# Differential attention: the low halves of eight weight chunks made by GpSimd in a stream of its own instead of by VectorE

## The reference, cut to what matters

```python
q = rms_norm((xn @ w_q).reshape(B, S, DIFF_HEADS, 2, DIFF_DH), q_gain) * (DIFF_DH ** -0.5)
...
s = jnp.einsum('bhcqd,bhckd->bhcqk', q_blk, k).astype(jnp.float32)
s = jnp.where(kpos[None, :] <= qpos[:, None], s, -jnp.inf)
p = jax.nn.softmax(s, axis=-1)
a = p[:, :, 0] - lam * p[:, :, 1]
return jnp.einsum('bhqk,bhkv->bhqv', a.astype(v.dtype), v)
...
o = rms_norm(o, head_gain) * (1.0 - lambda_init)
return o.reshape(B, S, DIFF_HEADS * DIFF_VD) @ w_out
```

## Time and profile before

| what | value |
|---|---|
| median of three executions | 2216.6 us (2216.18 to 2217.03) |
| the profiled execution | 2215.34 us |
| its span, first to last instruction | 2213.2 us |
| busy in the span: TensorE / VectorE / ScalarE / GpSimd | 2202.9 / 1624.5 / 1139.1 / 0.2 us |
| mean granted clock of TensorE | 1.000 of full speed |

### The profile page before, as it was taken

How to read it: one execution, slowest core, us unless ns; L and a number is a source line. 1 busy time by engine, 2 the same in 40 slices (tenths; PEclk the granted TensorE clock), 3 DMA queues, 4 the chain that set the end, 5 groups by cost and what they waited for, 6 DMA issues and landing times.

```text
span 2213.2 us, 32419 instructions
## 1 busy us (share of the span) xinstructions
PE 2202.9 (100%) x13130; PEld 1910.6 (86%) x13130; DVE 1624.5 (73%) x2428; ACT 1139.1 (51%) x1843; POOL 0.2 (0%) x4
## 2 busy tenths in 40 slices
PE   9999999999999999999999999999999999999999
PEld 7777999999778989998899888998987767898997
DVE  5755978797676969697777796686764777786774
ACT  5755644444475634355534473543555886543542
POOL 0000000000000000000000000000000000000000
PEclk9999999999999999999999999999999999999999
DMA  4222223232322223232311222222232112232222
GB/s 154 79 86 77 96 97 114 86 115 74 108 96 77 96 95 115 86 115 75 122 68 58 87 104 95 96 103 107 77 122 76 58 58 76 96 114 96 96 92 99
DMA packets 37300, 206.94 MB, mean 93 GB/s; under 512 B 4256, under 2 KB 4768, under 8 KB 17824
## 3 DMA queue, kind: packets, MB, share of 16 engines
q1 hardware_dynamic: 34560, 199.17, 25.2%
q10 hardware_dynamic: 2592, 5.70, 0.8%
HBM read 202.76 MB, written 2.10 MB: 93 GB/s over the span
## 4 chain that ended last, share of the span: by engine, by line
PE 97%; DVE 1%; ACT 1%; issue 0%; DMA 0%; ACTq 0%; DVEq 0%
PE ps L985 31%; PE ps L346 19%; PE ps L348 18%; PE ps L347 18%; PE ps L1510 2%; PE ps L2710 1%; PE ps L1565 1%; PE ps L1534 1%; PE ps L2241 1%; PE ps L1560 1%; PE ps L2729 1%; PE ps L1526 1%; PE ps L1216 0%; PE ps L2720 0%; PE ps L2267 0%
## 5 line engine op out<-in xcount | busy, mean ns | idle before, releaser
L422 DVE TENSOR_TENSOR low_w<-raw_w,high_w 128x2048 fp32r<-128x2048 f32 (+4 forms) x211 | 420.3, 1993 | 100.6 <-ACT high_w L401 100.3
L401 ACT ACTIVATE high_w<-raw_w 128x2048 fp32r<-128x2048 f32 (+4 forms) x211 | 352.1, 1670 | 147.9 <-DMA raw_w<-in_w_m_dn 93.9
L346 PE MATMUL ps<-ffn_hidh,high_w 128*128 128x512 f32 x864 | 336.6, 390 | 0.1
L347 PE MATMUL ps<-ffn_hidl,high_w 128*128 128x512 f32 x864 | 336.4, 389 | 0.0
L348 PE MATMUL ps<-ffn_hidh,low_w 128*128 128x512 f32 x864 | 336.2, 389 | 0.0
L985 PE MATMUL ps<-forms_th,forms_s 128*128 128x256 f32 x816 | 231.1, 283 | 0.0
L985 PE MATMUL ps<-xh,high_w 128*128 128x256 f32 x816 | 231.0, 283 | 0.0
L985 PE MATMUL ps<-xl,high_w 128*128 128x256 f32 x816 | 231.0, 283 | 0.0
L985 PE MATMUL ps<-xh,low_w 128*128 128x256 f32 x816 | 231.0, 283 | 0.0
L985 PE MATMUL ps<-forms_th,form_lows_s 128*128 128x256 f32 x816 | 231.0, 283 | 0.0
L985 PE MATMUL ps<-form_lows_t,forms_s 128*128 128x256 f32 x816 | 230.9, 283 | 0.0
(11 more groups left out here) (348 smaller groups left out, 4551.6 us busy)
## 6 DMA issues: line engine op xcount, KB each, us to landing
raw_w<-in_w_f_gu SPq DMA_DIRECT2D x44, 1024.0 KB, 4.7
raw_w<-in_w_m_up SPq DMA_DIRECT2D x32, 1024.0 KB, 4.8
raw_w<-in_w_m_dn SPq DMA_DIRECT2D x24, 1024.0 KB, 4.7
raw_w<-in_w_f_dn SPq DMA_DIRECT2D x8, 1024.0 KB, 4.7
raw_w<-in_w_m_dn SPq DMA_DIRECT2D x16, 512.0 KB, 3.4
raw_w<-in_w_b_qk SPq DMA_DIRECT2D x8, 1024.0 KB, 4.7
raw_w<-in_w_f_dn SPq DMA_DIRECT2D x8, 896.0 KB, 4.6
raw_w<-in_w_f_dn SPq DMA_DIRECT2D x16, 448.0 KB, 3.2
```

Source lines behind the costliest of these rows:

```text
L346: pe.matmul(out, sh, mh, start=start, stop=False)
L347: pe.matmul(out, sh, ml, start=False, stop=False)
L401: act.activation(wh[slot][:, 0:elems], raw[slot][:, 0:elems], ACT.Copy).then_inc(w_rounded, 1)
L422: dve.tensor_tensor(wl[slot][:, 0:elems], raw[slot][:, 0:elems], wh[slot][:, 0:elems].bitcast(F32), ALU.subtract).then_inc(w_split, 1)
```

## The change

The two calls of `split_weights` in `step` on VectorE are taken out. GpSimd gets a stream, `diff_pool`, which makes the same low halves for the 8 chunks from `st_diff.base + 2` to `st_bout.base + 1`, one 128x2048 subtraction for each, as soon as ScalarE has rounded the chunk. Chunks `st_diff.base` and `st_diff.base + 1` stay with VectorE ahead of the stage, and from `st_bout.base + 2` on VectorE makes all of them again, the first behind an added wait for GpSimd's last.

```diff
@@ step of diff_dve
             if past_two(p):
                 head_scale(p - 2)
-            if nx:
-                split_weights(dve, st_diff.base + p + 2)
             norm(p, st)
@@
             if not nx:
                 split(5)
-                split_weights(dve, st_diff.base + p + 2)
@@ tail of diff_dve
             split(6)
             head_low(p)
+            dve.wait_ge(w_split, st_bout.base + 2)
             split_weights(dve, st_bout.base + 2)
@@
         split_weights(dve, st_diff.base + 1)
+        prepared["dve"] = st_bout.base + 2
         attention_steps(NHD, project, step, tail)
+
+    def diff_pool(pool):
+
+        pool.wait_ge(w_split, st_diff.base + 2)
+        for c in range(st_diff.base + 2, st_bout.base + 2):
+            slot = c % NS
+            pool.wait_ge(w_rounded, c + 1)
+            if c > st_diff.base + 2:
+                pool.wait_ge(w_split, c)
+            pool.tensor_tensor(wl[slot][:, :], raw[slot][:, :], wh[slot][:, :].bitcast(F32),
+                               ALU.subtract).then_inc(w_split, 1)
@@
+    @block.gpsimd
+    def _(pool):
+        diff_pool(pool)
```

## The result

The changed kernel takes 2219.72 us (median of 22 executions, 2217.98 to 2222.14), the kernel before 2216.55 us (22 executions, 2215.41 to 2218.84). The ratio is 1.0015, 95% interval 1.0009 to 1.0020: 3.2 us or 0.15% slower. The interval leaves out 1, so a small loss is measured; it lies within the 0.2% that the prediction called the same. The profiled execution took 2219.80 us.

A forecast was written before the change was run, and what follows sets the result against it. TensorE, idle only 2.4 us of the 160 us stage, was taken as the bound. No gain in the steps and +3.0 us at the last chunk give 2218.3, plus the median's 1.3: 2219.6 us, range 2214.5 to 2222.5.

The forecast's parts named there:

- Part 1: Steps 0 to 6: taking seven splits off VectorE gains 0, covered by TensorE's own projection; at most 1.3 us.
- Part 2: GpSimd's subtraction takes 3.8 us, bounds 2.28 and 6.4; hidden in steps 0 to 6.
- the 3 to 5 us given as a sign: Trace after the change: GpSimd should show 8 subtractions of this length, the first seven beside the masks.
- Part 3: SBUF sharing: masks in middle steps undisturbed; last chunk holds VectorE's two-SBUF-operand instructions, at most GpSimd's whole instruction.
- The sum: Last step: tile 5's low half waits for GpSimd, delaying TensorE's matmul 3.65 us, head sum 2.95 us: +3.0 us, 2219.6 us.
- The variant: Last step: VectorE's tile 5 gets in before GpSimd, the head's low half waits instead, head sum at 1834.5: +1.65 us.
- Free: Rival: engines do not disturb each other, head sum in the last step 0.6 us earlier: -0.5 us, 2216.1 us; chance 0.32.
- The per-step collision: Rival: masks in each of seven steps also wait for GpSimd, 2.2 us a step, +18.4, 2235 us; chance 0.10.
- The gain from the freed VectorE: Rival: 1.3 us from steps 0 to 6 plus 0.6 us at the end, no disturbance: 2214.7 us; chance 0.08.

The follow-up runs named there:

- norm run: Changed kernel with GpSimd's first seven subtractions also waiting for the step's last exponential, so starting with VectorE's norm: 2247.30 us, ratio 1.0141 to the kernel before.
- write-only run: Changed kernel with GpSimd's last subtraction replaced by four chained memsets of the same tile, that chunk's low half left zero: 2220.93 us, ratio 1.0022.
- run in pieces: Changed kernel with GpSimd's last subtraction cut into four pieces of 512 columns, each waiting for the one before: 2219.93 us, ratio 1.0014.

## Why the prediction was right, point by point

**Part 1, no gain from the freed VectorE: right.** The norm came 0.9 us earlier in the step, the key scaling not, and the time went into its wait for TensorE (0.97 us, ended by L348). The kernel with seven chunks on GpSimd shows it without the loss: 2215.81 against 2216.33, a difference inside its interval.

**Part 2, GpSimd's duration: too small.** I took 3.8 us between 2.3 and 6.4; it is 4.6, and 5.29 for the last, outside the 3 to 5 us given as a sign. The figure of the Trainium skill, "GPSIMD Engine Reference", section 3.1, 4497 ns, was the better one: the trace has 4.59 to 4.61. In steps 0 to 6 it was hidden, as predicted, but with 0.6 us to spare ahead of L2968 (1730.08 to 1730.71) and not 1.4; in steps 0 and 1 it is 0.4 and 0.5 us.

**Part 3, the masks beside it and the last chunk colliding: right.** The masks kept their 0.29 to 0.69 us. The last chunk alone cost what the whole change cost. That the whole hold is paid and not a part of it, which the prediction called a judgement, came out so. By the Trainium skill, "SBUF — State Buffer", section "Who interferes with whom", a GpSimd instruction that reads SBUF holds a shared port pair for its whole length against VectorE instructions with two SBUF inputs or in a two-port mode, not against those with one, and one that only writes leaves two-input instructions alone. The traces agree for L2973 (3.43 us beside the subtraction, 1.53 us beside pieces of 1.27, 0.69 beside memsets) and for the masks, which are unchanged. They fit for the one-input `tensor_scalar` L3003 (4.48 us), if it is in a two-port mode. The rows do not show its mode. They show only that the same operation at L3005 goes through its columns at about twice the rate of the two-input L3012: 0.28 to 0.48 us against 0.34 to 0.75 us, from 128 to 512 columns. One place does not follow from who started first: L3025, whose record began after GpSimd's and which was not held.

**The sum, +3.0 us: right in size, composed wrongly, and so partly by luck.** Two of its steps failed and made up for each other. I let tile 5's low half wait for GpSimd, with the other order as a variant at +1.65. The variant is what happened: GpSimd's record begins at 1830.04, but L3025 at 1830.23 went through in its usual 0.69 us, and GpSimd's instruction was 0.69 us longer for it. The variant's price was 0.5 us low, the wait costs 2.2: GpSimd's job took 0.8 us longer than assumed, and 0.3 us of that was won back at its two ends (against tile 5's matmul it ended 0.6 us later than in the variant, and the low half ended 0.55 us behind it, not 0.7). And the sum took every matmul behind the wait at full rate. The clock's fall, which the sum did not have, added 1.6 us in the profiled execution and about 1.2 in the median (3.2 us of loss against 2.0 with TensorE kept busy). The wait of 2.2 us from the traces and this 1.2 make 3.4 us, and 3.2 was measured. With the right duration but its own order and no fall of the clock, the sum would have been +3.8 us, 2220.4 us.

**The rivals.** Free fell with the change's own trace, and with the run of the eighth chunk alone. The per-step collision did not come in this kernel, but it is real in another place: with GpSimd at the norm it costs up to 4.8 us a step, more than the 2.2 us that I had for the masks. The gain from the freed VectorE (2214.7 us) did not come: at most 0.5 us, which no interval tells from nothing.

## What to carry to other kernels

Here GpSimd's subtraction was free where it lay, over its whole length, beside VectorE instructions with one operand in PSUM and one in SBUF (masks, q scaling). Beside instructions with two operands in SBUF, and beside a `tensor_scalar`, VectorE lost up to GpSimd's whole remaining time. So look at which VectorE instruction falls into its time at each of its places, the last one in the loop included, rather than at its slack. Seven of eight places were safe by 0.4 to 0.6 us, and the eighth cost 3.2 us. And where one engine bounds the kernel, ask first how long it is idle in the stage (2.4 us of 160 here): that is all that help for another engine can win, while a new wait of 2 us can also cost the clock.

## What the runs showed of the hardware that was not expected

- A held VectorE instruction shows as a long one, however small it is: 4.48 us for 128x4 elements, 3.43 us for 128x512. The view of waits blames VectorE for TensorE's wait; GpSimd is named there as the cause of nothing.
- When GpSimd's record began (1830.04), VectorE was in a two-operand instruction (L3012); the next one, L3025, followed without a gap and passed GpSimd, whose own instruction became 0.69 us longer. It was so in the change, with only the last chunk moved, and at the norm run's last step (5.28 to 5.29 us each). All of this is one place in the program; why is not shown.
- Behind an idle stretch of TensorE the clock fell in some cases and not in others, at like lengths. It fell (matmuls of 0.63 us, 0.43 apart) behind 2.63 us in the change, behind 3.49 us in the write-only run, behind 2.5 to 3.3 us in six steps of the run at the norm, and behind 1.69 us, with 0.73 us shortly before it, in the run in pieces. It stayed at full speed behind 2.63 us in the run with the eighth chunk alone and in the last step of the run at the norm, and behind 1.61 and 0.90 us close together in that run's first step. Idle stretches of 0.5 to 0.7 us by themselves never did this. What decides is not shown.
